# Order of PE's work in the first chunks: squares summed ahead of the group products, group products ahead of blocks that wait for a chain

## The reference

```
mod = silu(c) @ ada_w[l] + ada_b[l]                 # 1024 x 6144
sh1, sc1, gt1, sh2, sc2, gt2 = split(mod, 6)
h = rms_norm(x, norm1_g[l]) * (1 + sc1) + sh1
proj = h @ w_in[l]                                  # then attention, convolution, gates ...
```

## Time and profile before

| | us |
|---|---|
| median of 3 runs | 995.46 (994.81 to 996.46) |
| the profiled execution | 995.31 |
| its span, first to last instruction | 993.5 |
| PE busy | 965.8 (97%) |
| DVE busy | 760.6 (77%) |
| ACT busy | 519.6 (52%) |
| mean granted TensorE clock | 0.992 |

### The profile page before, as it was taken

One profiled execution on the slowest core, in us unless ns is written; L12 is line 12 of the kernel. 1 busy time (PEld: TensorE's weight loads), 2 busy tenths in 40 slices (PEclk: granted clock), 3 DMA queues, 4 the chain that ended last, 5 costly groups with the idle time before them and its releaser, 6 DMA issues.

```text
span 993.5 us, 18813 instructions
## 1 busy us (share of the span) xinstructions
PE 965.8 (97%) x7795; PEld 909.8 (92%) x7795; DVE 760.6 (77%) x1138; ACT 519.6 (52%) x728; POOL 18.1 (2%) x23
## 2 busy tenths in 40 slices
PE   5999999999999999999999999999999999999997
PEld 3799899999888999999989989999988899999997
DVE  3459899976686788889885799999658578888734
ACT  3384456557345566654255644665744455565432
POOL 5000000000000000000000000000000000000001
PEclk9899999999999999999999999999999999999999
DMA  9976364556693556957994534444769445555551
GB/s 315 325 236 218 106 196 154 190 188 234 233 335 128 171 182 199 339 170 276 395 335 128 168 105 136 152 132 136 237 229 356 155 150 190 170 185 171 197 170 43
DMA packets 140979, 202.05 MB, mean 203 GB/s; under 512 B 3416, under 2 KB 114148, under 8 KB 140900
## 3 DMA queue, kind: packets, MB, share of 16 engines
q1 hardware_dynamic: 140564, 200.68, 60.2%
q10 hardware_dynamic: 336, 0.21, 0.1%
HBM read 199.83 MB, written 1.05 MB: 202 GB/s over the span
## 4 chain that ended last, share of the span: by engine, by line
PE 88%; DVE 7%; DMA 1%; issue 1%; ACT 1%; SPq 1%; DVEq 0%; ACTq 0%
PE PB L1460 19%; PE PB L1462 18%; PE PB L1461 18%; PE PB L1483 2%; PE SC L1460 2%; PE SC L1462 2%; PE SC L1461 2%; PE PB L1484 2%; PE PB L1485 2%; DVE wL L964 2%; DVE buf L1073 1%; PE MI L1413 1%; DMA ada_pre<-in_ada_w 1%; PE ST L1520 1%; PE OB L1462 1%
## 5 line engine op out<-in xcount | busy, mean ns | idle before, releaser
L1460 PE MATMUL PB<-hH,wH 128*128 128x256 f32 x1360 | 389.8, 287 | 0.0
L964 DVE TENSOR_TENSOR wL<-raw,wH 128x2048 fp32r<-128x2048 f32 (+3 forms) x152 | 323.2, 2127 | 85.6 <-ACT wH L676 81.3
L1462 PE MATMUL PB<-hH,wL 128*128 128x256 f32 x1360 | 384.8, 283 | 0.0
L1461 PE MATMUL PB<-hL,wH 128*128 128x256 f32 x1360 | 384.7, 283 | 0.0
L676 ACT ACTIVATE wH<-raw 128x2048 fp32r<-128x2048 f32 (+3 forms) x152 | 268.4, 1782 | 118.4 <-DMA raw<-in_w_down 53.1
L1460 PEld LDWEIGHTS PB<-hH,wH 128*128 128x128 f32 x1360 | 260.6, 192 | 6.9 <-issue 6.6
L1461 PEld LDWEIGHTS PB<-hL,wH 128*128 128x128 f32 x1360 | 260.7, 192 | 0.8 <-issue 0.7
L1462 PEld LDWEIGHTS PB<-hH,wL 128*128 128x128 f32 x1360 | 260.6, 192 | 0.0
L1073 DVE SCALAR_TENSOR_TENSOR buf<-G,vec,buf 128x256 f32<-128x256 f32 x240 | 98.2, 479 | 0.3
L1262 DVE SCALAR_TENSOR_TENSOR ups<-PB,vec,ups 128x254 f32<-128x254 f32 (+1 forms) x176 | 72.7, 475 | 19.7 <-ACT ups L835 19.6
L835 ACT ACTIVATE ups<-PB,vec 128x256 f32<-128x256 f32 x88 | 44.9, 561 | 27.5 <-PE PB L1462 19.8
(11 more groups left out here) (282 smaller groups left out, 1690.6 us busy)
## 6 DMA issues: line engine op xcount, KB each, us to landing
raw<-in_w_in SPq DMA_DIRECT2D x48, 1024.0 KB, 5.4
raw<-in_w_up SPq DMA_DIRECT2D x44, 1024.0 KB, 5.1
ada<-in_ada_w SPq DMA_DIRECT2D x40, 1024.0 KB, 8.6
raw<-in_w_down SPq DMA_DIRECT2D x22, 1024.0 KB, 5.0
ada_pre<-in_ada_w SPq DMA_DIRECT2D x8, 1024.0 KB, 13.5
raw<-in_w_o SPq DMA_DIRECT2D x8, 1024.0 KB, 8.5
raw<-in_w_out_diff SPq DMA_DIRECT2D x4, 1024.0 KB, 5.5
raw<-in_w_out_conv SPq DMA_DIRECT2D x4, 1024.0 KB, 6.7
```

The source lines that it names most:

```text
L964: dve.tensor_tensor(wL[s][:, 0:size], raw[s][:, 0:size], wH[s][:, 0:size].bitcast(F32), ALU.subtract).then_inc(w_lo[s], 1)
L1460: pe.matmul(out, a, xh(k), start=first and k == 0, stop=False, skip_group_check=True)
L1461: pe.matmul(out, a, xl(k), start=False, stop=False, skip_group_check=True)
L1462: ins = pe.matmul(out, b, xh(k), start=False, stop=last and k == kt - 1, skip_group_check=True)
```

## The change

On PE, `norm_sum(0, 0)` moves ahead of the first group's products. `collect(1)` moves behind `first_chunk(0, 0)`; `group_products(2, 0)` moves ahead of `first_chunk(0, 1)`; `first_chunk(0, 2)` moves ahead of `group_products(3, 1)`; `first_chunk(1, 2)` moves ahead of `collect(3)`. On ACT, `root(0, 0)` moves ahead of `group_evict(0)`. DVE's, POOL's and SP's lists stay as they are, and no instruction is added or dropped.

```
             for l in range(LAYERS):
                 evict_first(l)
+            root(0, 0)
             group_evict(0)
-            root(0, 0)
             high(0, 0)
...
+            norm_sum(0, 0)
             group_products(0, 0)
             group_products(0, 1)
-            norm_sum(0, 0)
             after(x_ready, DT)
             collect(0)
             group_products(1, 0)
             group_products(1, 1)
+            first_chunk(0, 0)
             collect(1)
-            first_chunk(0, 0)
+            group_products(2, 0)
             first_chunk(0, 1)
-            group_products(2, 0)
             group_products(2, 1)
             first_chunk(1, 0)
             collect(2)
             group_products(3, 0)
             first_chunk(1, 1)
+            first_chunk(0, 2)
             group_products(3, 1)
-            first_chunk(0, 2)
+            first_chunk(1, 2)
             collect(3)
-            first_chunk(1, 2)
             first_chunk(0, 3)
             first_chunk(1, 3)
```

## The result

The changed kernel takes 998.54 us (median of 7, 998.20 to 999.93), the kernel before 995.60 in the same comparison (7, 994.77 to 996.46). The ratio is 1.0031, 95% interval [1.0020, 1.0043]: slower by 0.31%, 2.9 us between the medians. The profiled execution took 998.33 us, its span is 996.5 against 993.5.

A forecast was written before the change was run, and what follows sets the result against it. PE bounds the kernel, busy 965.8 of 993.5 us; its main loop was put 2.5 us later, so the median 995.46 + 2.5 = 998.0 us, range for 8 in 10 994.9 to 999.7.

The forecast's parts named there:

- passed on one to one: A shift of PE's first main-loop product, at 48.40 us before, reaches the kernel's end in full: +2.5 us.
- three signs of being wrong: Clock 1.00 around 25 to 31 us; collect(1) not later than before; main loop's first shift differing from the end's.
- Part 1, squares first: norm_sum starts at 11.70 us, reciprocal ends at 17.7; group 0 gains 2.5 us, both its hL ready near 24.1.
- Part 2, `collect(1)` behind 12 products: first_chunk(0, 0) starts at 24.8, 2.4 us earlier; collect(1) waits until 27.45, group 1's chain is 2.0 us later.
- the sum: PE's start-up timeline with clock back at 35.5: first_chunk(1, 0) at 35.8, +1.2 us; main loop at 50.9, +2.5 us.
- The clock's return at 35.5: PE's early half clock ends at 35.5 us, nearly midway between bounds 33.0 and 37.5; between 34 and 37: 0.50.
- unbroken work starts only at 31.7: PE's row of products without waits, 27.17 us before, begins at 31.7; 5.8 us later gives the late bound, 37.5.
- at 33 or earlier: Rival: early half clock ends at 33.0 as before; main loop at 50.4, +2.0 us, time 997.5; chance 0.22.
- Part 3, the chain laid bare: first_chunk(1, 2) no longer covers 1.5 us of collect(3)'s 2.4 us chain; main loop at 50.9, +2.5 us in all.
- from there both kernels do the same pieces at the full clock: From first_chunk(1, 0) to the main loop PE runs at clock 1.00; the last two chunks take 3.02 us.
- no half clock: Rival: clock doesn't fall, or is back before 25 us; main loop at 47.6, -0.8 us, time 994.7; chance 0.14.
- nothing that comes by the clock on the wall holds PE: From the main loop's start at 48.40 us, weights load when PE returns buffers and every chain hangs on PE products.

The follow-up runs named there:

- Parts 1 and 2 together: The changed kernel with group_products(3, 1) back ahead of first_chunk(0, 2) and collect(3) back ahead of first_chunk(1, 2): 996.62 us, ratio 1.0013 to the kernel before.
- the experiment in which the half clock did last from 22.4 to 32.7 with no second fall: The changed kernel plus 16 dropped products behind collect(3) and 9 in PE's wait for W at TD3: 996.54 us, ratio 1.0014 to the kernel before.
- `warm`: Kernel before with squares and root first, collects early with products on both sides, six dropped products in PE's early transfer waits: 997.63 us, ratio 1.0025.

## Why the prediction was right

The forecast was 998.0 and slower; 998.54 was measured. The direction and the places came as worked out, the size did not: it came out near by luck. At the main loop +2.5 us was forecast and the profile has +1.56; passed on one to one that is 997.0. The missing 1.4 us came from a spell of half clock near 625 us that the forecast doesn't have. Of its three signs of being wrong two showed in that profile, in part: the clock was 1.00 from 28.2 us on, and the shift at the main loop (1.56) isn't the shift of the end (3.0).

DVE's timeline in the first profile of the changed kernel, for the first two parts:

```profile
15.53 1.75 DVE L1305 RECIPROCAL rdev<-rdev 128x256 f32<-128x256 f32 x1 [3.26 <-ACT rdev L689]
...
23.13 2.23 DVE L989 SCALAR_TENSOR_TENSOR hL<-xn,mod,hH 128x256 fp32r<-128x256 f32 x2
...
30.29 0.89 DVE L989 SCALAR_TENSOR_TENSOR hL<-xn,mod,hH 128x256 fp32r<-128x256 f32 x2 [0.18 <-ACT hH L703]
32.49 2.29 DVE L964 TENSOR_TENSOR wL<-raw,wH 128x2048 fp32r<-128x2048 f32 x1 [1.32 <-ACT wH L676]
```

*Part 1, squares first: right.* The reciprocal ended at 17.3 (17.7 forecast); alone, the part is worth nothing (0.9996). `hL` of group 0 took 2.2 us, not 0.9, in a stretch in which POOL was working too, but its first half was in time: `first_chunk(0, 0)` started at 24.82 (24.8 forecast).

*Part 2, `collect(1)` behind 12 products: the place right, the price too high.* It started at 27.55 (27.45 forecast). `hL` of group 1 came at 31.2 and `wL` of chunk 1 at 34.8 (31.7 and 35.3), and PE waited 1.13 and 1.27 us for them (0.4 and nothing forecast). `first_chunk(1, 0)` started at 34.84 against 34.59: +0.25 us, where the sum had +1.2. The products ran at the full clock again, and the rest went into waits. Parts 1 and 2 together cost 1.3 us by the medians (996.62), but 0.1 us at the main loop in the profile of that kernel.

*The clock's return at 35.5: wrong.* It rose at 28.2 and at 27.3 in two profiles, and in the second it fell again from 30.7 to 34.1. The step that failed here is "unbroken work starts only at 31.7": by the forecast's own times PE has no wait from 22.8 to 31.3, as `first_chunk(0, 0)` follows the second product of group 1 at once, and the profile shows none from 22.95 to 29.8. So the case "at 33 or earlier" held in the first profile: main loop at 49.96, where I had 50.9 for the forecast and 50.4 for that rival. In the experiment in which the half clock did last from 22.4 to 32.7 with no second fall, the main loop was at 50.61 and +2.21; the rival's sum was +2.0.

*Part 3, the chain laid bare: right in the first profile, short by half in two others.* `collect(3)` at 43.86, wait 2.12 us (2.3 forecast). From `first_chunk(1, 0)` to the main loop it took 15.12 us (15.1 forecast), 1.3 more than before. The step that doesn't hold in every execution is "from there both kernels do the same pieces at the full clock": behind a bare wait of 2.1 us the clock fell in two of three profiles of the changed order, and the last two chunks took 4.5 us instead of 3.0. Filling that wait with 16 useless products gave 1.5 to 2 us of 3.1 back.

*Passed on one to one: right for the shift, incomplete.* No wait later in the list absorbs or adds to the 1.56 us. What came on top in the first profile was 1.4 us of half clock near 625. That fall is in 4 of the 11 profiles in which `TD3`'s wait wasn't filled, among them one with the end order of before; it isn't in the one profile of the kernel before, nor in the three in which that wait was filled. Whether the change makes it more frequent stays open. So the right number has two errors in it that cancel: half clock early, which I put too long, and half clock late, which I left out.

The rival on the other side, "no half clock", was tested with `warm`: its sum of -0.8 us didn't come true either, even with the full clock and a better order. It left out the transfer of chunk 3; "nothing that comes by the clock on the wall holds PE" was true of the kernel before only by some 0.8 us (51.56 to 52.37).

## What to carry to other kernels

Put the small product that starts a chain through other engines as early as its input allows, and count the work left behind it: here moving 1.5 us of products from behind `collect(3)` to ahead of it laid 1.4 us bare, and that part alone cost 4 us. Price a PE wait like this one, of 2.1 us, at more than its length: in three of the four profiles that have it bare, the products behind it ran at half clock and took 1.5 us more. And before a start-up phase is polished, look at what lands next: chunk 3's transfer, which landed at 48.6 us before, left room for about 0.8 us only.

## What the runs showed that I hadn't expected

Useless products made a kernel faster: 16 of them in a wait of 2.1 us, 1.5 to 2 us of 998. The clock's return can't be read off the order of work: in six profiles with the early order of the changed kernel PE starts an unbroken row of work at about 23 us, and the clock rose at 26.2, 26.9, 27.3, 27.6, 28.2 and 32.7 us. And the same kernel showed its second spell of half clock at 47.8 us in one execution and at 625.5 in another, so one profile can't tell what a spell costs a kernel: that took a filled wait and its timed median.
